# First stage of a transformer block on one Trainium2 core: two modulation column groups summed on TensorE, and products started before the last rows are transposed

## What is computed

```python
c_act = jax.nn.silu(c)
mod = c_act @ ada_w[layer] + ada_b[layer]
sh1, sc1, g1, sh2, sc2, g2 = [m[:, None, :] for m in jnp.split(mod, 6, axis=-1)]
h = rms_norm(x) * (1.0 + sc1) + sh1
proj = h @ w_in                      # q, k, v, o and 8 gate columns
```

## Times and profile before

| | us |
|---|---|
| median of 3 runs | 1136.0 |
| lowest and highest of them | 1135.12, 1844.59 |
| the profiled execution | 1137.11 |
| span in its trace | 1135.3 |

### The profile page before, as it was taken

The page is one execution under the profiler, slowest core; times in us unless marked ns, Lnnn a source line. Parts: engine busy times, 40 slices in busy tenths (PEclk is TensorE's granted clock), DMA queues, the critical chain, the costliest instruction groups (busy, mean ns, idle before and its releaser), DMA issues.

```text
span 1135.3 us, 16846 instructions
## 1 busy us (share of the span) xinstructions
PE 1103.3 (97%) x6093; PEld 959.9 (85%) x6093; DVE 694.2 (61%) x1172; ACT 432.6 (38%) x767; POOL 183.3 (16%) x151
## 2 busy tenths in 40 slices
PE   4999999999999999999999999999999998999997
PEld 4798899899898899988888888888888886888886
DVE  5956716617518844676785767666756456744676
ACT  6763212222223431354343433343334316344344
POOL 5632302302404731730000000000000000000000
PEclk9999999999999999999999999999999998999999
DMA  9415413414414532112645264536453889665553
GB/s 366 158 61 199 140 59 115 151 37 135 147 38 149 186 112 91 78 38 75 212 143 192 97 210 139 187 101 213 139 174 114 289 301 342 197 188 201 187 166 149
DMA packets 87195, 178.17 MB, mean 157 GB/s; under 512 B 8121, under 2 KB 31289, under 8 KB 86097
## 3 DMA queue, kind: packets, MB, share of 16 engines
q1 hardware_dynamic: 86416, 175.07, 45.7%
q0 software_dynamic: 704, 2.13, 0.6%
HBM read 137.02 MB, written 40.16 MB: 156 GB/s over the span
## 4 chain that ended last, share of the span: by engine, by line
PE 90%; DVE 4%; POOL 2%; DMA 1%; issue 1%; ACT 1%; SPq 0%; DVEq 0%; POOLq 0%; ACTq 0%
PE OP L2054 26%; PE OP L1825 17%; PE O L2054 15%; PE ST L2054 5%; PE DC L2054 5%; PE AD L2054 5%; PE O L1825 4%; PE ST L1825 3%; PE AD L1825 2%; PE DC L1825 2%; PE O L2011 1%; PE O L2012 1%; PE DC L2016 1%; PE ST L1854 1%; DMA ada<-ada_first 1%
## 5 line engine op out<-in xcount | busy, mean ns | idle before, releaser
L1825 PE MATMUL OP<-wH,hH 128*128 128x256 f32 x640 | 184.9, 289 | 0.4 <-issue 0.4
L1825 PE MATMUL OP<-wH,hL 128*128 128x256 f32 x640 | 181.2, 283 | 0.0
L1825 PE MATMUL OP<-wL,hH 128*128 128x256 f32 x640 | 181.2, 283 | 0.0
L1608 DVE TENSOR_TENSOR dL<-dF,dH 128x1024 fp32r<-128x1024 f32 x77 | 92.5, 1222 | 74.0 <-ACT dH L1080 73.4
L1825 PEld LDWEIGHTS OP<-wH,hH 128*128 128x128 f32 x640 | 122.5, 191 | 3.4 <-issue 3.2
L1825 PEld LDWEIGHTS OP<-wL,hH 128*128 128x128 f32 x640 | 122.6, 192 | 0.0
L1825 PEld LDWEIGHTS OP<-wH,hL 128*128 128x128 f32 x640 | 122.5, 191 | 0.0
L1080 ACT CAST dH<-dF 128x1024 fp32r<-128x1024 f32 x77 | 79.6, 1053 | 95.9 <-DMA dF<-w_units 42.3
L2054 PE MATMUL OP<-tH,wsH 128*128 128x512 f32 x264 | 103.0, 390 | 0.0
L2054 PE MATMUL OP<-tH,wsL 128*128 128x512 f32 x264 | 102.8, 390 | 0.0
L2054 PE MATMUL OP<-tL,wsH 128*128 128x512 f32 x264 | 102.8, 389 | 0.0
(11 more groups left out here) (310 smaller groups left out, 2665.9 us busy)
## 6 DMA issues: line engine op xcount, KB each, us to landing
raw<-w_units SPq DMA_DIRECT2D x76, 512.0 KB, 4.5
dF<-act_mid SPq DMA_DIRECT2D x77, 256.0 KB, 2.8
ada<-ada_rest SPq DMA_DIRECT2D x64, 256.0 KB, 2.8
wst<-w_units SPq DMA_DIRECT2D x44, 256.0 KB, 4.8
down_mid<-wst SPq DMA_DIRECT2D x22, 512.0 KB, 3.2
dF<-down_mid SPq DMA_DIRECT2D x44, 256.0 KB, 2.9
dF<-w_units SPq DMA_DIRECT2D x33, 256.0 KB, 5.6
ada<-ada_first SPq DMA_DIRECT2D x8, 1024.0 KB, 10.6
```

The costliest lines, as they stand in the source:

```text
L1608: nc.vector.tensor_tensor(dL[g][:], dF[g][:], dH[g][:].bitcast(F32), ALU.subtract).then_inc(d_L, 1)
L1825: ins = nc.tensor.matmul(out_ap, lhs[a], rhs[b], start=(n == 0 and i == 0), stop=(last and i == 2))
```

## The change

Four things change, all in the first 65 us.

1. Groups 0 and 1 (`DIRECT = 2`) are no longer summed on VectorE. `direct_columns(k)` on TensorE takes the weights as they were loaded: for each of the 2 columns 8 matmuls, each with a 128x128 slice of `ada0` as the stationary operand and one column of silu(c) as the moving one, accumulated in `DC`. It stands behind the transposes of row 1 (k = 0) and of row 3 (k = 1).
2. Blocks (0, 0) and (1, 0) are multiplied in the midst of the rows: behind the transposes of row 5 and of row 6. The order of the blocks (`M_SEQ`) is (0,0), (1,0), (0,1), (1,1), then as before.
3. VectorE scales all 8 rows, GpSimd none. The transposes go to other banks, `XT_BANKS = [ST[1], O[1], OP[1], AD]`. `AD` is also the bank of `sum1`, so `sum1(2)`, the first of now six, waits until the last transposes are copied out. TensorE's `mod_columns(k + 2)` stands within block (k, 1), behind its first three matmuls.
4. SP issues the weights of group 1 behind row 3, and the first half unit behind row 4. Groups 4 and 5 wait for `direct_columns` instead of for sums.

The diff, cut to its core (the renumbered waits of `low1`, `modulate` and `shift` are left out):

```diff
-POOL_ROWS = (2, 3, 4)
-DVE_ROWS = tuple(t for t in range(NT) if t not in POOL_ROWS)
-HN1 = len(DVE_ROWS)
+DIRECT = 2
+M_SEQ = [(0, 0), (1, 0), (0, 1), (1, 1)] + [(k, half) for k in range(2, KD) for half in range(2)]
+M_AT = {kh: n for n, kh in enumerate(M_SEQ)}
...
-        XT_BANKS = [ST[0], ST[1], O[0], O[1]]
+        XT_BANKS = [ST[1], O[1], OP[1], AD]
...
-                if k >= 4:
-                    sp.wait_ge(acc0_ok, N1 * (k - 3))
+                if 4 <= k < 4 + DIRECT:
+                    sp.wait_ge(mod1_mm, k - 3)
+                elif k >= 4:
+                    sp.wait_ge(acc0_ok, N1 * (k - 3 - DIRECT))
...
-                if t == 5:
+                if t == 3:
+                    ada_first_tile(1)
+                if t == 4:
                     load_unit(0, (0,))
-            for k in range(1, KD):
+            for k in range(2, KD):
...
-            for t in POOL_ROWS:
-                norm1(t)
             first_high(0)
             first_low(0)
...
                 root(t)
-                if t == 5:
+                if t == 3:
                     act.wait_ge(b1_ok, 1)
                     mod_columns(0)
-            modulate(0, 0)
+                if t == 5:
+                    modulate(0, 0)
+                    mod_columns(1)
+                if t == 6:
+                    modulate(1, 0)
             evac_xT(NT - 2)
+            act.wait_ge(xT_ok[1], NT - 2)
+            evac_xT(NT - 2, 1)
             evac_xT(NT - 1)
             modulate(0, 1)
-            act.wait_ge(xT_ok[1], NT - 2)
-            evac_xT(NT - 2, 1)
             evac_xT(NT - 1, 1)
-            for k in range(1, KD):
+            modulate(1, 1)
+            for k in range(DIRECT, KD):
...
-                if k:
-                    dve.wait_ge(acc0_ok, k * N1)
+                base = (k - DIRECT) * N1
+                if base:
+                    dve.wait_ge(acc0_ok, base)
+                else:
+                    dve.wait_ge(xT_ok[1], NT)
...
             for t in range(NT):
-                if t == 2:
-                    sum1(0)
                 inverse(t)
+                norm1(t)
                 if t >= 2:
                     evac_xT(t - 2)
-                if t not in POOL_ROWS:
-                    norm1(t)
-                if t == NT - 1:
+                if t == NT - 2:
                     low1(0, 0)
-            for k in range(1, KD):
+            for k in range(DIRECT, KD):
                 sum1(k)
...
+            def direct_columns(k):
+
+                pe.wait_ge(c_act, 1)
+                pe.wait_ge(ada0_in[k], 16)
                 if k:
                     pe.wait_ge(mod1_ok, 2 * k)
+                for m in range(2):
+                    for r in range(KD):
+                        ins = nc.tensor.matmul(DC[:, 2 * k + m:2 * k + m + 1], ada0[:, k, r, m * P:(m + 1) * P],
+                                               cact[:, r:r + 1], start=(r == 0), stop=(r == KD - 1))
+                ins.then_inc(mod1_mm, 1)
...
+                    for m in range(2):
+                        ins = three(QK_BANKS[2 * half + m][:], tuple(w[:, k, m * DK:(m + 1) * DK] for w in ws),
+                                    hs, k, k, last)
                         if last:
-                            ins.then_inc(gates_mm, 1)
-                        if k == 0 and half == 0:
-                            mod_columns(1)
+                            ins.then_inc(qk_mm, 1)
+                        if half and m == 0 and k + DIRECT < KD:
+                            mod_columns(k + DIRECT)
...
+                for t in range(NT):
+                    x_transposes(t)
+                    if t in (1, 3):
+                        direct_columns(t // 2)
+                    if t == 5:
+                        first_step(0, 0)
+                    if t == 6:
+                        first_step(1, 0)
+                for k, half in M_SEQ[2:]:
+                    first_step(k, half)
```

More of the change, by code:

```diff
@@ L645, in _ @@
             pool.wait_ge(m_L, 1)
[L646 to L650, removed]
+            for k, half in M_SEQ[1:]:
+                low1(k, half)
+                if (k, half) == (1, 1):
                     first_high(1)
-                if k == 2:
+                if (k, half) == (2, 1):
                     first_low(1)
-            pool.wait_ge(acc0_ok, N1 * KD)
+            pool.wait_ge(acc0_ok, N1 * (KD - DIRECT))
             nc.gpsimd.memset(rows[0:GATE_ROWS, A_, :], 0.0).then_inc(rows_set, 1)
@@ L1871, in start, with x_transposes @@
                 pe.wait_ge(const_ok, 2)
[L1872 to L1876, removed]
+                ws = unit_weights(0, 2 * DK)
+                def x_transposes(t):
+                    pe.wait_ge(n_hn, t + 1)
                     for j in range(2):
@@ L1883, in start @@
                         ins.then_inc(n_tr, 1)
[L1884 to L1891, removed]
-                        mod_columns(k + 1)
-                    for half in range(2):
-                        pe.wait_ge(m_L, 2 * k + half + 1)
-                        if k == 0:
-                            pe.wait_ge(xT_ok[half], NT)
-                        hs = h_cols(half)(k)
-                        last = k == KD - 1
-                        for m in range(2):
-                            ins = three(QK_BANKS[2 * half + m][:], tuple(w[:, k, m * DK:(m + 1) * DK] for w in ws),
-                                        hs, k, k, last)
-                            if last:
-                                ins.then_inc(qk_mm, 1)
-                        for i in range(2):
-                            ins = nc.tensor.matmul(OP[half][:], gate_weights[:, k, :], hs[i], start=(k == 0 and i == 0),
-                                                   stop=(last and i == 1))
-                        if last:
-                            ins.then_inc(gates_mm, 1)
-                        if k == 0 and half == 0:
-                            mod_columns(1)
@@ new lines, in first_step @@
+                def first_step(k, half):
+                    pe.wait_ge(m_L, M_AT[k, half] + 1)
+                    if k == 0 and half == 0:
+                        pe.wait_ge(wg_L, 1)
+                        pe.wait_ge(w_L, 1)
+                    elif k == 0:
+                        for j in range(2):
+                            pe.wait_ge(xT_ok[j], NT)
+                    elif k == 4 and half == 0:
+                        pe.wait_ge(w_L, 2)
+                    hs = h_cols(half)(k)
+                    last = k == KD - 1
+                    for m in range(2):
+                        ins = three(QK_BANKS[2 * half + m][:], tuple(w[:, k, m * DK:(m + 1) * DK] for w in ws),
+                                    hs, k, k, last)
+                        if last:
+                            ins.then_inc(qk_mm, 1)
+                        if half and m == 0 and k + DIRECT < KD:
+                            mod_columns(k + DIRECT)
+                    for i in range(2):
+                        ins = nc.tensor.matmul(OP[half][:], gate_weights[:, k, :], hs[i], start=(k == 0 and i == 0),
+                                               stop=(last and i == 1))
+                    if last:
+                        ins.then_inc(gates_mm, 1)
```

26 lines of the change are left out of this document (12 added, 14 removed).

## The result

| | us |
|---|---|
| the change, median of 4 runs (1143.13 to 1151.85) | 1147.6 |
| the kernel before, on the same chip | 1135.8 |
| ratio, 95% interval | 1.0097 (1.0076 to 1.0117) |
| the profiled execution of the change, its span | 1145.78, 1144.0 |

The change is slower by 1.0%, 11.8 us in the medians, inside the 2% within which it was forecast. The number forecast was 1150.3. Between the two profiled executions the span grew by 8.7 (1135.3 to 1144.0).

The account below looks back on a forecast made before the run. TensorE's blocks and VectorE's sums were taken to end the stage together, 36.4 us after X. The move of X, 11.3, plus the clock, 3.0, made 14.3 on 1136.0, so 1150.3 us; range 1140 to 1156.

Parts of the forecast that it names:

- The change is worth the move of X: Behind row 7's transposes: distance to the stage's end stays 36.4 us, early blocks' and sums' savings paid back by late sums.
- X: Start of row 7's transposes, the last row turned: 28.4 us before, forecast 39.7, a move of 11.3.
- the stage: First part of the kernel, ending when the first product of values of head 0 starts, at 64.76 us before.
- I take 6.9: Direct columns on TensorE between the rows: 32 load-and-matmul pairs at 0.215, 6.9 us per group at the low level.
- sign of being wrong: Named signs: X under 31, pairs at 0.11, or stage time not reaching the end one for one.
- the quick case: Rival for the direct columns: 3.5 us each, X at 33.0, time 1142.6, range 1139 to 1146; chance 0.22.
- the main case: Direct columns at 0.215 a pair, X at 39.7, time 1150.3, own range 1146 to 1156; chance 0.66.
- together 3: Clock falls on TensorE: 1.5 us in blocks (0, 0) and (1, 0), the rest behind row 7; between 0 and 7.
- Time saved or lost in the stage reaches the end one for one: Behind the stage TensorE works in a row: an end of the stage d later moves the kernel's end by d.
- The "faster" rival: Sums following X at once end the stage some 2.5 us earlier for the same X, 1133.5; chance 0.06.

Follow-up runs that it names:

- late blocks: The change with blocks (0, 0) and (1, 0) multiplied behind row 7's transposes: 1140.97 us, ratio to the kernel before 1.0064.
- early copies: The change with ScalarE copying the last transposes out of PSUM ahead of `modulate(0, 1)`: 1143.85 us, ratio to the kernel before 1.0052.
- the sums freed: The change with both early blocks behind row 7 and transposes in the banks of before, leaving `AD` free: 1138.54 us, ratio to the kernel before 1.0030.
- a quarter: The change with 2 of the 8 matmuls of each direct column, 8 pairs a group instead of 32: 1144.38 us, ratio to the kernel before 1.0072.
- twice the columns: The change with each direct column computed twice, 64 pairs a group: 1154.55 and 1163.12 us, ratio to the kernel before 1.0195.
- the late sum: The kernel before with its second sum (group 1) waiting until the last transposes are copied out: 1141.07 us, ratio 1.0034.
- the last one: The kernel before with VectorE scaling all rows and the first `low1` on GpSimd: 1133.78 us, ratio 0.9972.
- the two last versions of before: The kernel before with VectorE scaling all rows, 1134.34 us; the same with the first `low1` on GpSimd too, 1133.78 us.

## Why the prediction was right, and where it was not

**The change is worth the move of X: right.** The distance from X to the end of the stage was 36.4 by the forecast. It measured 36.93, 36.75 and 36.87 in three traces of the change, 36.87 with late blocks, 36.13 with early copies, 35.89 with the sums freed, 36.80 and 36.59 with a quarter and with twice the columns; before it was 36.39 and 36.71. X alone moved between 28.6 and 45.1. The working behind it holds too: the first sum 3.3 behind X for the 3.6 forecast, and TensorE's wait for it inside block (0, 1), 40.90 - 33.87 = 7.0 for 7.5. That the two early blocks gain nothing behind X is shown: late blocks leave the distance where it was. That the sums' late start is what pays it back is shown for the old order, where the late sum costs 5.0, and only in part for the new one: a start 1.5 earlier brought 0.6 to 0.8. Early blocks with sums that follow X at once, for which the prediction named 2.5, were not run.

**"I take 6.9": right as a size at the low level, wrong for every trace of the unedited change.** The step that failed is "the direct columns follow transposes, like the `mod_columns` at 21.03, which had transposes on both sides and still ran at the slow pace", and with it the chances of 0.66 against 0.22. All three traces of the change show 3.7 to 4.1, which is the prediction's own sign of being wrong, pairs near 0.11. The other price, 6.83, stands in the trace with the copies moved. Which one an execution gets hangs on when the clock first rises: at 11.3, 11.8 and 12.3 in the three traces, at 37.4 in that one. The trace of before had its first rise at 30.6, but that is one execution: the second trace of the same kernel rose at 12.4. Of twelve executions of the change the lower heap has seven, near where the quick case was put (mean 1144.6 for 1142.6; six of the seven in its range of 1139 to 1146), and the upper five, where the main case was (1151.0 for 1150.3, 1146 to 1156). That the upper heap is the slow pairs rests on four things: with a quarter of the pairs none of six executions is there, with twice the pairs the two executions lie 8.6 apart, the mean granted clocks of the heap (0.993 to 0.995) lie around that of the trace with slow pairs (0.994), and that trace is of an execution near it (1148.2, with the copies moved). No trace of the unedited change in the upper heap was caught, and some 2 us stay open: with the 0.7 that the moved copies save, the slow trace accounts for 1149, not 1151.0. The median 1147.6 lies between the heaps and describes neither; that it is within 2.7 of the forecast 1150.3 is luck.

**The rule of 107 ns for a load, weighed there.** 32 pairs in 6.83 are 0.213 a pair at the low level; in the quick case, mostly at the high level, they are 0.12 to 0.13. The rule of the Trainium skill, page "TensorE: Matmul & The Clock Gate", section "LDWEIGHTS (loading the stationary operand)", which names no clock beside its figure, fits the second alone. The prediction decided for two prices, and that was right; by the page's figure alone the forecast would have been the quick case.

**Quick columns, X at 33.0: off by up to 1.65.** X was 31.35, 31.49 and 33.87. The rival was laid out for one pace of everything else; the transposes and blocks ahead of X take up to 2.5 more or less with the clock. The stage end in it, 69.4 by 33.0 + 36.4, stands between the 68.1 and 70.8 measured.

**The clock, "together 3": wrong as a sum, and the agreement of X is luck.** Half of it, 1.5, was charged ahead of X to blocks (0, 0) and (1, 0). With slow columns block (0, 0) did run at the low level, 3.58 from 32.86 to 36.44 for the 2.3 laid out, but it began 1.0 earlier than the 33.9 forecast and row 6 was turned in 1.3 for 1.7, and so X met the 39.7 that had no clock in it. The other half was charged behind X. The fall came where it was put (38.6 to 45.4 in the change, 44.2 to 51.1 with the copies moved), but the distance grew by 0.5 at most, and in the trace with slow columns not at all: its stage ended at 75.78 for the forecast 79. The sum charged 13 products at the low level and took off only 1.2 for the wait for `sum1(3)`. In that stretch TensorE is waiting for VectorE: the next sum comes 3.8 after the last, whatever TensorE's pace, so the slower products run into a wait that shrinks. In all three traces of the change TensorE no longer waits for `sum1(3)`. Most of this was a cost beside other work, counted as one on the path.

**Time saved or lost in the stage reaches the end one for one: only within 2 to 3 us.** Traces of the change had 2.5 to 2.9 more at the end than at the stage's end (6.04 to 8.69, 3.34 to 5.86, 3.61 to 6.52), that with slow columns 0.1 more (11.02 to 11.16), the kernel before with all rows on VectorE 1.7 (-3.97 to -2.25), the unedited kernel before 2.5 (-0.47 to 2.06); the other six lie between 0 and 2.4. All are differences to one trace of before, which did not wait at 940 as its repeat did. Of the change's two steps that near 109 stands in all three of its traces, but with the same 0.6 also in two versions of before (the late sum and the last one); that at 379 in two. What puts them there is open.

**The "faster" rival** asked for X at 28.4. It was approached only without the early blocks (28.58, 65.45) and with the sums freed as well (64.90), level with 64.76 and no better. What speaks for it in the prediction, that rows 2 to 4 no longer wait for GpSimd, is real and worth 4 us of the stage by itself; the change spends it on the later landings and the two `modulate` ahead of rows 6 and 7, on early blocks, and, where the clock rises late, on direct columns. That this part could be a gain alone was not asked in the prediction.

## What to carry to other kernels

Work moved ahead of the last item of a pipeline is worth only what it shortens behind it: find the instruction from which the rest runs at a fixed distance (here row 7's transposes), and count first how far the move delays that. A price read early in one trace can have a second value: here a load and its matmul took 0.213 or 0.11, by when the clock first rose. Look for both in other executions, and forecast two heaps rather than one. Of a change with several parts, test each alone: here one line of it (`POOL_ROWS = ()`) gained 0.2% in the old kernel while the whole lost 1%.

## What the runs showed of the hardware

**The clock rose with transposes alone ahead of it.** In the change TensorE had done only fp32 transposes, busy from 8.41 on, when the granted clock rose at 11.3. In the kernel before with the late sum it rose at 10.7, with nothing but transposes from 7.99 on; in the second trace of before at 12.4, 0.5 behind the last of them. The Trainium skill, page "TensorE: Matmul & The Clock Gate", section "Part 4: PE-mode transpose", says that the full clock doesn't engage for TensorE's transpose mode; these traces disagree for `nc.tensor.transpose` of fp32 blocks, though no row names the mode (such a transpose shows as one load and one matmul, a plain fp32 matmul as two of each). In other executions of the same transposes it did not rise before 30.6 (before) and 37.4 (the change with the copies moved).

**The clock fell while one-column products ran.** In the change it fell at 14.7 and at 21.5 with the direct columns running without a gap (3.40 of 3.40 us busy ahead of either fall), and in the trace with the copies moved two runs of 6.83 us went by without a rise, TensorE busy 6.60 of 6.60 us in each.

**The clock column shows 1.00 ahead of the first record,** while pairs take 0.213 and transposes 1.73 a row. The pace of known instructions tells the level, the column doesn't.

**VectorE's scaling of a row stretches beside GpSimd,** though GpSimd no longer scales. It took 0.74 or 0.75 for most rows, but 1.65 for row 5 and 2.87 for row 4 in the two last versions of before, more than the 1.53 that the prediction took as the most. The second of these, both engines:

```profile
17.40 2.35 POOL L621 TENSOR_TENSOR wL<-raw,wH 128x1024 fp32r<-128x1024 f32 x1
17.43 2.87 DVE L1252 TENSOR_SCALAR xin<-xin,rstd 128x1024 f32<-128x1024 f32 x1
```

Each long scaling began while GpSimd split the first half weight unit, and ended 0.55 or 0.56 behind the end of that split: 20.30 behind 19.75 here, 20.46 behind 19.90 for the 1.65, 21.88 behind 21.32 for a scaling of 1.05 in the first trace of the change, 22.13 behind 21.58 for one of 1.35 with the copies moved. So the rows read as a wait for GpSimd's instruction to end, at the price of what is left of it, and 1.53 was no bound. The instruction was not moved away, so this is not tested.
